# Split float32r matmuls replaced by plain float32 matmuls in a small hybrid transformer, one core

## The reference, cut to what matters

```python
for l in range(2):
    h = rmsnorm(x, g_mix[l])
    if l == 0:      # 4 retention heads and 4 stick-breaking (SB) heads of 128, one in and one out projection
        y = mixer_ab(h, ..., w_in_ab, ..., w_out_ab, ...)
    else:           # h @ cv_w1 (1024 -> 2048), gate, 31-tap depthwise conv, layernorm, silu, @ cv_w2
        y = conformer_conv(h, ...)
    x = x + y
    x = x + cross_attn(rmsnorm(x, g_cross[l]), mk, mv, xa_wq[l], xa_wo[l])   # mk, mv = mem @ xa_wk, mem @ xa_wv
    x = x + conv_ffn(rmsnorm(x, g_ffn[l]), ffn_w_up[l], ..., ffn_w_down[l])  # 1024 -> 5632, 3 taps, 2816 -> 1024
y = rmsnorm(x, g_final)
```

## Time and profile before

| | us |
|---|---|
| median of 2 runs (3767.76 to 3770.43) | 3769.1 |
| span of the profiled execution | 3769.6 |
| TensorE busy | 3405.0 (90%) |
| TensorE weight loads busy, beside it | 3050.0 (81%) |
| VectorE busy | 1930.9 (51%) |
| GpSimd busy | 1006.6 (27%) |
| ScalarE busy | 790.2 (21%) |

### The profile page before, as it was taken

How to read it: one execution, slowest core, us unless ns; L and a number is a source line. 1 busy time by engine, 2 the same in 40 slices (tenths; PEclk the granted TensorE clock), 3 DMA queues, 4 the chain that set the end, 5 groups by cost and what they waited for, 6 DMA issues and landing times.

```text
span 3769.6 us, 48282 instructions
## 1 busy us (share of the span) xinstructions
PE 3405.0 (90%) x19230; PEld 3050.0 (81%) x19230; DVE 1930.9 (51%) x2589; ACT 790.2 (21%) x1024; POOL 1006.6 (27%) x452
## 2 busy tenths in 40 slices
PE   5999899699989799999997888798989799999997
PEld 5777788497849799999997777496948799999996
DVE  5443555623241655455457899833251555545546
ACT  3664111201110221121122100121120222112111
POOL 2111211040203233333332322030302233333331
PEclk9999999799979899999998999899979899999998
DMA  2001333424041111111112100003132111111111
GB/s 108 34 34 61 102 123 112 130 73 144 23 176 48 38 45 46 46 45 46 46 45 51 34 22 22 24 34 135 33 143 75 38 45 46 46 45 46 46 46 68
DMA packets 83606, 237.74 MB, mean 63 GB/s; under 512 B 15722, under 2 KB 20714, under 8 KB 81522
## 3 DMA queue, kind: packets, MB, share of 16 engines
q1 hardware_dynamic: 74962, 217.96, 17.3%
q10 hardware_dynamic: 8480, 17.32, 1.2%
HBM read 217.93 MB, written 17.32 MB: 62 GB/s over the span
## 4 chain that ended last, share of the span: by engine, by line
PE 76%; DVE 16%; issue 4%; ACT 2%; DMA 1%; SPq 0%; DVEq 0%; ACTq 0%
PE ps L402 59%; DVE ca L1171 7%; PE ps L751 2%; PE ps L658 2%; PE ps L715 2%; PE ps L669 1%; PE ps L689 1%; PE ps L733 1%; DVE Hl L1167 1%; DVE rst L1195 1%; PE ps L492 1%; PE ps L505 1%; DVE acc L1167 1%; PE ps L482 1%; DVE hf L1171 1%
## 5 line engine op out<-in xcount | busy, mean ns | idle before, releaser
L378 POOL TENSOR_TENSOR Wh<-wraw,con 128x1024 fp32r<-128x1024 f32 x224 | 431.8, 1928 | 2696.7 <-PE ps L402 2663.3
L402 PE MATMUL ps<-Hh,Wh 128*128 128x344 f32 x4320 | 958.1, 331 | 121.4 <-DVE Hl L1167 74.4
L402 PE MATMUL ps<-Hl,Wh 128*128 128x344 f32 x4320 | 927.0, 323 | 0.0
L402 PE MATMUL ps<-Hh,Wl 128*128 128x344 f32 x4320 | 922.0, 322 | 0.0
L402 PEld LDWEIGHTS ps<-Hh,Wh 128*128 128x128 f32 x4320 | 738.5, 191 | 163.3 <-issue 141.0
L402 PEld LDWEIGHTS ps<-Hl,Wh 128*128 128x128 f32 x4320 | 740.6, 191 | 0.0
L402 PEld LDWEIGHTS ps<-Hh,Wl 128*128 128x128 f32 x4320 | 729.7, 190 | 0.0
L1171 DVE SCALAR_TENSOR_TENSOR cb<-ub,fp,cb 128x1024 f32<-128x1024 f32 x176 | 405.5, 2304 | 572.2 <-ACT cb L867 572.2
L381 POOL TENSOR_TENSOR Wl<-wraw,Wh 128x1024 fp32r<-128x1024 f32 x224 | 574.7, 2566 | 17.6
L1167 DVE TENSOR_TENSOR X<-ps,X 128x1032 f32<-128x1032 f32 x200 | 245.8, 1229 | 351.0 <-PE ps L402 351.0
L1171 DVE SCALAR_TENSOR_TENSOR ca<-uu,cpar,ca 128x1024 f32<-128x1024 f32 x184 | 285.8, 1553 | 6.3
(11 more groups left out here) (198 smaller groups left out, 2935.9 us busy)
## 6 DMA issues: line engine op xcount, KB each, us to landing
wraw<-in_wts SPq DMA_DIRECT2D x224, 512.0 KB, 3.3
pg<-in_ck SPq DMA_DIRECT2D x64, 256.0 KB, 2.8
pg<-in_cv SPq DMA_DIRECT2D x64, 256.0 KB, 2.8
mw<-in_memw SPq DMA_DIRECT2D x32, 512.0 KB, 3.3
cc<-in_cmk SPq DMA_DIRECT2D x16, 1024.0 KB, 6.8
cc<-in_cmv SPq DMA_DIRECT2D x16, 1024.0 KB, 5.0
X<-in_x SPq DMA_DIRECT2D x8, 1032.0 KB, 7.0
out_y<-X ACTq DMA_DIRECT2D x8, 516.0 KB, 3.0
```

Source lines behind the costliest of these rows:

```text
L378: pool.tensor_tensor(Wh[:, j, :], wraw[:, j, :], one.broadcast_to((P, 1024)), ALU.mult).then_inc(w_hi, 1)
L402: ins = mm(o, w[:, wcol[0], wcol[1]:wcol[1] + P], r, start=first and a == 0, stop=last and a == 2)
```

## The change

All 224 weight tiles are multiplied by plain float32 matmuls, one for each three. GpSimd's splits, ScalarE's copies to Hh and Gh, and VectorE's subtractions to Hl and Gl are gone. SyncE loads straight into the tile that TensorE reads (`wt`, two slots), as soon as the tile two before it is done. Norms write Hn directly, the FFN's product goes straight to G, cross attention's output is written by ScalarE alone. C has its own place, so X stays in SBUF and is not loaded again. In a retention head the four weight loads move from behind page loads 1, 1, 9, 9 to 1, 3, 9, 13.

```diff
 def weight(t, slot, first=False):
     if not first:
-        sp.wait_ge(w_split, t - 1)
-    load(wraw[:, slot:slot + 1, :], wts[...], w_raw[slot])
+        sp.wait_ge(tile_done, t - 1)
+    load(wt[:, slot:slot + 1, :], wts[...], w_raw[slot])
...
-for j, behind in enumerate((1, 1, 9, 9)):
+for j, behind in enumerate((1, 3, 9, 13)):
...
-for c in range(KC // 2):
-    sp.wait_ge(ss("c_lo"), 2 * c + 2)
-    load_x(c)
...
-def split(t, j, landed, first=False):
-    pool.wait_ge(w_raw[j], landed)
...
-def three(outs, wcol, xs, first, last):
-    for a, (w, x) in enumerate(((Wh, 0), (Wh, 1), (Wl, 0))):
-        for o, r in zip(outs, xs[x]):
-            ins = mm(o, w[:, wcol[0], wcol[1]:wcol[1] + P], r,
-                     start=first and a == 0, stop=last and a == 2)
...
+def chunk(slot, s, k, src):
+    for g in range(GRP):
+        ins = mm(ps[:, 3 * s + g, 0:GN], wt[:, slot, k * P:(k + 1) * P],
+                 src[:, k, g * GN:(g + 1) * GN], start=k == 0, stop=k == KC - 1)
...
-pe.wait_ge(w_split, t + 1)
+pe.wait_ge(w_raw[slot], 16 * pair + 16)
...
-return lambda k: pe.wait_ge(ss("n_lo"), KC * nk + k + 1)
+return lambda k: pe.wait_ge(ss("n_hf"), KC * nk + k + 1)
...
-product(T_OUT, 4, F_OUT, lambda k: pe.wait_ge(ss("c_lo"), k + 1))
+product(T_OUT, 4, F_OUT, lambda k: None, C)
...
-        pe.wait_ge(*of_layer(l, "x_ol", 2 * u))
+        pe.wait_ge(*of_layer(l, "x_oh", 2 * u))
...
-pe.wait_ge(*of_layer(l, "g_lo", 2 * i + 2))
+pe.wait_ge(*of_layer(l, "f_gm", 2 * i + 2))
...
-        tt_(gf[:, :], cb[:, 0, :], cb[:, 1, :], ALU.mult, ss("f_gm"))
+        tt_(ff["G"][:, par, k, :], cb[:, 0, :], cb[:, 1, :], ALU.mult, ss("f_gm"))
-        dve.wait_ge(*of_layer(l, "g_hi", 2 * i + (k + 1)))
-        tt_(ff["Gl"][:, par, k, :], gf[:, :], ff["Gh"][:, par, k, :].bitcast(F32), ALU.subtract, ss("g_lo"))
```

More of the change, by code:

```diff
@@ L396, in _, with weights_in, tile, first_pair @@
             mm = pe.matmul
-            def three(outs, wcol, xs, first, last):
-                for a, (w, x) in enumerate(((Wh, 0), (Wh, 1), (Wl, 0))):
-                    for o, r in zip(outs, xs[x]):
-                        ins = mm(o, w[:, wcol[0], wcol[1]:wcol[1] + P], r,
-                                 start=first and a == 0, stop=last and a == 2)
[L404 to L412, removed]
+            def chunk(slot, s, k, src):
+                for g in range(GRP):
+                    ins = mm(ps[:, 3 * s + g, 0:GN], wt[:, slot, k * P:(k + 1) * P],
+                             src[:, k, g * GN:(g + 1) * GN], start=k == 0, stop=k == KC - 1)
                 if k == KC - 1:
                     ins.then_inc(tile_done, 1)
-            def tile(t, slot, s):
-                pe.wait_ge(w_split, t + 1)
+            def weights_in(slot, pair):
+                pe.wait_ge(w_raw[slot], 16 * pair + 16)
+            def tile(pair, slot, s, src=Hn):
+                weights_in(slot, pair)
                 for k in range(KC):
-                    chunk(slot, s, k)
-            def first_pair(t, ready):
+                    chunk(slot, s, k, src)
+            def first_pair(t, ready, src=Hn):
                 behind = KC // 2
-                pe.wait_ge(w_split, t + 2)
+                for s in range(2):
+                    weights_in(s, t // 2)
                 for k in range(KC + behind):
@@ L429, in first_pair, with product @@
                         ready(k)
-                        chunk(0, 0, k)
+                        chunk(0, 0, k, src)
                     if k >= behind:
-                        chunk(1, 1, k - behind)
-            def product(t0, npairs, freed, ready):
+                        chunk(1, 1, k - behind, src)
+            def product(t0, npairs, freed, ready, src=Hn):
                 for s in range(2):
                     pe.wait_ge(set_free[s], freed + 1)
-                first_pair(t0, ready)
+                first_pair(t0, ready, src)
                 with pe.Fori(1, npairs) as i:
@@ L462, in _ @@
             pe.wait_ge(ss("sb_ev"), 1)
-            tile(T_SB + 2, 0, 0)
+            tile(T_SB // 2 + 1, 0, 0)
             with pe.Fori(0, 2) as i:
@@ L638, in head @@
                 end_stage(pe, end_pe, i + (E_SB + 1))
-            tile(T_RET + 3, 1, 0)
+            tile((T_RET + 3) // 2, 1, 0)
             with pe.Fori(0, H - 1) as i:
@@ L1018, in _ @@
             head(H - 1, False)
-            for c in range(KC):
-                fn(Hh[:, c, :], C[:, c, :], ACT.Copy, ss("c_hi"))
             squares(1, F_OUT)
@@ L1085, in ffn, with pair @@
                 norm(nk)
-                def pair(i, k, par, t, first):
+                def pair(i, k, t, first):
                     for v in range(2):
@@ L1154, in _ @@
             ffn(1, E_FF1, 5, T_FFN1, F_FF1)
-            norm(6, hi=False)
+            norm(6)
             for c in range(KC):
@@ L1190, in sum_square, with norm @@
                     tt_(acc[:, :], acc[:, :], sq[:, c % 2, :], ALU.add, ss("n_acc"))
-            def norm(nk, gcol, split=True, between=lambda c: None):
+            def norm(nk, gcol, dst=Hn, between=lambda c: None):
                 dve.wait_ge(ss("n_rt"), nk + 1)
@@ L1475, in turned @@
                     copy(at["pT"][:, u % 2, 1, :], ps[:, 5, :], ss("x_pt1"))
-                def out(u):
-                    hx, half = u // 2, u % 2
-                    for dc in range(2):
-                        dve.wait_ge(*of_layer(l, "x_oh", 2 * u + dc + 1))
-                        cols = slice(512 * half, 512 * half + 512)
-                        tt_(Hl[:, 2 * hx + dc, cols], ps[:, 6 + dc, :], Hh[:, 2 * hx + dc, cols].bitcast(F32),
-                            ALU.subtract, ss("x_ol"))
                 maxima(0)
@@ L1682, in _ @@
             ffn(1, E_FF1, 5, T_FFN1, F_FF1)
-            norm(6, PCOL["g_final"], split=False)
+            norm(6, PCOL["g_final"], X)
 _OUTS = {
```

125 lines of the change are left out of this document (38 added, 87 removed).

## The result

The changed kernel takes 4215.06 us (median of 2 runs, 4212.67 to 4217.45), against 3769.1 before: a ratio of 1.118, with a 95% interval from 1.115 to 1.122. The profiled execution has a span of 4210.9 us, 441.3 more than before. The forecast was +468.3.

A forecast was written before the change was run, and what follows sets the result against it. TensorE, 76% of the chain, was taken as the bound. Terms FFN +297.2, SB +33.8, retention +36.6, OUT +18.2, cross attention +78.8, conv -12, W2 +15.7 sum to +468.3 on 3769.6: about 4238 us, range 4190 to 4290.

The forecast's parts named there:

- the chunk's price: Weight matmuls, one 128-row contraction slice: three plain matmuls at 290.5 ns a record, 1.743 us, +0.323 us over nine split ones.
- FFN: Both FFN stages: a section goes from 70.3 to 84.1 us, 0.4 of it waiting; +297.2 us for both layers.
- Retention heads: Retention stage: 13 longer tiles +33.6 us, pages queued behind tiles +3.0, together +36.6 us.
- the step on SyncE's order: Retention heads: next tile's load waits for a tile to end, pages stand behind it; nearly covered, 1 us a head.
- SB: SB stage: four heads +31.0 us, tile 2 ahead of them +2.6, first pair +0.2; +33.8 us.
- Start: First tile pair after a norm: VectorE writes Hn faster than TensorE eats, TensorE starts about 2.5 us sooner.
- Conv: Conv stage: VectorE's taps quicken without GpSimd, TensorE becomes the limit at 39.95 us a block; -12 us with first pair.
- Cross attention and OUT: Cross attention: WQ and WO +20.7 us each, waits -2.0, both layers +78.8; OUT: 2.5 sooner, chunks +20.7, +18.2.
- 1: Weight matmuls: load and matmul pair sets the time, a plain pass costs 158 ns; about 2935 us, chance 2%.
- 2: Retention heads: pages queue behind tiles, costing 7 to 12 us a head; about 4265 us, chance 12%.
- 3: Head borders, cross attention, FFN sections: waits shrink more with GpSimd quiet, conv gives 16; about 4210 us, chance 12%.
- a quiet GpSimd helps only where VectorE is waited for: Shared port pair: GpSimd and VectorE lock each other out; so quiet GpSimd gives rival 3 no more than 26 us.

The follow-up runs named there:

- Experiment 4: Changed kernel with each plain matmul of 344 columns cut into two of 172; 4247.84 us, ratio 1.127.
- Experiment 5: Changed kernel with GpSimd again doing two 128x1024 operations for each weight tile, their results unused; 4250.62 us, ratio 1.128.
- experiment 2: Changed kernel with a retention head's four weight loads behind pages 3, 7, 9, 15 instead of 1, 3, 9, 13; 4203.75 us, ratio 1.115.
- experiment 1: Changed kernel with the rope and page table loads put ahead of SB's last two weight loads; 4196.05 us, ratio 1.113.
- experiment 6: The kernel before, with only the conv's 16 W1 tiles plain and unsplit; 3755.97 us, ratio 0.9964.
- experiment 7: The kernel before, with each split matmul of 344 columns cut into two of 172; 7187.83 us, ratio 1.907.

## Why the prediction was right, and where it was off

The sum was 27 us too high in span, 23 against the median, 5 to 6% of the difference. The mechanism was right: two records for each plain matmul, priced by columns, on an engine that was the limit. That the total came so near is in part luck. Three costs were missed or too small: the wait at the border (7.3 us), the clock behind it (4.4), and pages behind tiles (3.6). They stand against four gains that were missed or too small: the record's price (14), the FFN's wait (8), the sums of squares at stage ends (13) and the start (4). That is 15 against 39, and leaves some 3 us of the 27 open. Point by point:

- **Two records, by columns** (the chunk's price): shown. It was sized 1.3 ns too high a record, since L839's 12.31 us had an end to take off that I estimated at 0.1 us (42 records of 289.2 ns leave 0.16). 10752 x 1.3 = 14 us, half of the miss and the main one. Experiment 4 confirms that a record costs columns and 2.5 ns. The Trainium skill (FP8 and Floating Point Precision, TensorE Precision Notes) gives true FP32 four passes; 2 x 289.2 = 578 ns are 4.04 column times at 2.4 GHz, so the trace agrees. A 4 : 3 ratio by counting passes would still have been wrong, 578.4 : 473.4 is 1.22, and +22% was measured where nothing but products stands: 111.06 us against 90.91.
- **FFN**: a section takes 83.28, not 84.1. 0.4 us of wait kept in each of 20 sections was 8 us too many. Two reasons were given for the end of the wait, the quiet GpSimd and the longer down product (3.47 us, 27.76 / 8). Experiment 5 points to the second: VectorE's delay is back in amount and the wait is not. It does not show it, since the delay falls on other instructions. The stage of layer 0 gained 2.7 us more, at its end, through the sums of squares.
- **Retention heads**: +38.3 against 31.5, and here the step on SyncE's order was incomplete. Pages behind tiles cost 6.6 us in three heads (experiment 2), not 3.0. The other miss stands at the border: the prediction followed the page loads past the moved weight load, and not the rope and page tables in the same queue. They cost 7.3 us of wait and 4.4 of clock (experiment 1). The wait falls between the two stages, and so shows in SB's row of the table.
- **SB**: +43.3 against 38.9 with tile 15. With the 7.3 us of that wait taken away, the stage is 2.9 below the forecast. The forecast gave a quiet GpSimd nothing here, and experiment 5 puts 12.3 us back with a busy one. The rows of VectorE say why the two differ: its GpSimd work delays VectorE by 31 us in this stage, the splits by some 9. So the 12.3 us are no measure of what the splits cost here; that the splits cost the 2.9 fits, and is not shown: two executions of the same instructions differ by 2.6 us in this stage (experiment 2).
- **Start**: -6.1 against -2.5. In experiment 5 it is 3.7 later, so the extra gain is GpSimd's silence during the norm: two sums of squares take 2.93 and 3.19 us before, and 1.24 in the change.
- **Conv**: -11.0 against -12, through the mechanism that was named: GpSimd leaves, VectorE's taps stop to be the limit, TensorE's 39.78 us (forecast 39.95, and 40.2 in its sum) take over. Experiment 5 puts 15.6 us back by GpSimd alone, and experiment 6 gets 8.3 with W1's splits alone gone.
- **Cross attention and OUT**: 2.5 to 4 us a stretch below the forecast. The record's price explains 384 x 1.3 = 0.5 us of a product. In OUT and from WO to FFN the sums of squares cover the rest (2.7). From WQ to WO some 3 us a layer stay open; in layer 0 TensorE's wait for the softmax weights p fell from 4.2 to 1.8 us there.
- **Rivals.** 1 fell with the change itself (289.2 ns a record). 2 was real and small. 3 was right that waits would shrink by more: the FFN's wait, the stage ends and the start are 25 us that the sum did not have, which would have made its 26, and the costs at the border and of the pages hid more than half of it. That the total ended 5 us above its 4210 owes as much to the record's price. The sentence that a quiet GpSimd helps only where VectorE is waited for holds by places (1 us in an FFN, 15.6 in conv), and the sum's list of places was too short: the start and five stage ends belonged on it. The Trainium skill (SBUF — State Buffer, its bullets on the shared port pair) has the two engines shut each other out; the trace agrees with 0.68 against 2.84 us for one operation.

## What to carry to other kernels

Price a change of data type by what a pass costs on the chain at the kernel's own column count, and not by counting passes: here six plain records of 289 ns stood against nine split ones of 158. What such a change takes off the other engines is worth something only where they are waited for, and one stage that is bound by them may deserve it alone: that version was the only one to beat the kernel before. When the event that releases a load moves, follow every load behind it in the same queue up to the next stage, small tables too: a wait of 7.3 us came from two of them, and cost more than half as much again in clock. And look for a slowed engine at the ends of stages, where the others wait for its last instructions: 13 us stood there, in five places.

## What was not expected of the hardware

- Splitting a product into narrower matmuls is nearly free for plain float32 (145.8 ns for 172 columns, against 289.2 for 344) and dear for split float32, 111.6 ns against 157.8: the same product takes 128.62 us in place of 90.91.
- The granted clock stood at 0.50 for 2028 us on end while TensorE was busy without a gap (213.4 ns a pass in experiment 7). High busy time alone did not bring back the 2.4 GHz level here. Cause open.
- Why a split pass of 344 columns takes 157.8 ns, 14.5 above its columns, where a plain one takes 2.5 above them, stays open: a floor of 111.6 ns does not reach it.
